# A depthwise convolution moves from VectorE to GpSimd, and a block of zero-writes moves later

## The reference

```python
def causal_depthwise_conv(u, w, b):          # u: 512 tokens x 768 channels, w: 4 taps
    out = lax.conv_general_dilated(u, w[:, None, :], window_strides=(1,),
        padding=[(CONV_WIDTH - 1, 0)], dimension_numbers=('NWC', 'WIO', 'NWC'),
        feature_group_count=u.shape[-1])
    return out + b

def first_block(x, w_in, conv_w, conv_b, ...):
    proj = jnp.einsum('bsd,de->bse', x, w_in[l])
    q, k, v, iq, ik, iw, z, xbc, dt_raw = jnp.split(proj, IN_SPLIT_POINTS, axis=-1)
    ...
    att = dsa_attention(q, k, v, iq, ik, iw * INDEXER_SCALE, topk)   # top 128 keys per query
    xbc = jax.nn.silu(causal_depthwise_conv(xbc, conv_w, conv_b))    # inside ssd_mixer
    ...
    mixed = jnp.einsum('bse,ed->bsd', jnp.concatenate([att, ssd], -1), w_out[l])
```

## Time and profile before

| what | value |
|---|---|
| median of three runs | 2731.35 us |
| the profiled execution, its own time | 2729.13 us |
| its span | 2727.3 us |
| TensorE busy | 2595.5 us (95%) |
| VectorE busy | 1299.9 us (48%) |
| ScalarE busy | 1090.7 us (40%) |
| GpSimd busy | 837.0 us (31%) |
| DMA | 318.80 MB, 117 GB/s on the mean |
| granted TensorE clock, mean | 0.978 |

### The profile page before, as it was taken

How to read it: one execution, slowest core, us unless ns; L and a number is a source line. 1 busy time by engine, 2 the same in 40 slices (tenths; PEclk the granted TensorE clock), 3 DMA queues, 4 the chain that set the end, 5 groups by cost and what they waited for, 6 DMA issues and landing times.

```text
span 2727.3 us, 30622 instructions
## 1 busy us (share of the span) xinstructions
PE 2595.5 (95%) x12190; PEld 2075.9 (76%) x12190; DVE 1299.9 (48%) x1841; ACT 1090.7 (40%) x1696; POOL 837.0 (31%) x354
## 2 busy tenths in 40 slices
PE   7998999999899999989999999999999999999997
PEld 6777787777676788878788888766888878788886
DVE  2895456777548646544431010576457353610113
ACT  2344235566426547333322122347374233322232
POOL 3300010000131344432234444321444432344344
PEclk9998989999999999999999999999999999999999
DMA  6242238899621233341223323221333331233332
GB/s 205 86 108 60 74 135 287 312 354 343 200 74 47 62 93 101 95 130 62 78 77 109 108 92 102 71 62 33 100 93 101 109 108 55 70 100 116 93 93 77
DMA packets 220078, 318.80 MB, mean 117 GB/s; under 512 B 17185, under 2 KB 176033, under 8 KB 219809
## 3 DMA queue, kind: packets, MB, share of 16 engines
q1 hardware_dynamic: 201184, 284.24, 32.7%
q10 hardware_dynamic: 16592, 24.72, 2.7%
q0 software_dynamic: 2160, 7.89, 0.8%
HBM read 301.06 MB, written 15.75 MB: 116 GB/s over the span
## 4 chain that ended last, share of the span: by engine, by line
PE 87%; DVE 8%; ACT 2%; issue 1%; DMA 1%; ACTq 0%; POOL 0%; DVEq 0%; SPq 0%
PE ps L639 80%; PE ps L790 4%; PE ps L651 3%; DVE stats L2061 1%; DVE rows L2071 1%; DVE pair_l L2356 1%; DMA rows<-in_x 1%; DVE x_lo L1987 1%; DVE xc L2217 0%; DVE shift L2090 0%; DMA xblk<-xs 0%; ACT pair_h L1665 0%; ACT w_hi L1438 0%; DVE rows L2083 0%; DVE qf L2447 0%
## 5 line engine op out<-in xcount | busy, mean ns | idle before, releaser
L603 POOL TENSOR_TENSOR w_lo<-w_raw,w_hi 128x1024 fp32r<-128x1024 f32 x331 | 814.8, 2472 | 1512.2 <-ACT w_hi L1438 1512.1
L639 PE MATMUL ps<-x_hi,w_hi 128*128 128x512 f32 x1624 | 656.4, 404 | 19.0 <-DVE x_lo L1987 16.5
L639 PE MATMUL ps<-x_lo,w_hi 128*128 128x512 f32 x1624 | 640.0, 394 | 0.0
L639 PE MATMUL ps<-x_hi,w_lo 128*128 128x512 f32 x1624 | 637.7, 393 | 0.0
L1438 ACT ACTIVATE w_hi<-w_raw 128x1024 fp32r<-128x1024 f32 x331 | 340.5, 1052 | 459.3 <-PE ps L639 447.8
L639 PEld LDWEIGHTS ps<-x_hi,w_hi 128*128 128x128 f32 x1624 | 308.1, 190 | 103.7 <-issue 19.4
L639 PEld LDWEIGHTS ps<-x_lo,w_hi 128*128 128x128 f32 x1624 | 307.7, 189 | 71.0
L639 PEld LDWEIGHTS ps<-x_hi,w_lo 128*128 128x128 f32 x1624 | 308.3, 190 | 67.1 <-issue 2.9
L2591 DVE TENSOR_TENSOR fhd<-fsg,ps 128x512 f32<-128x512 f32 x44 | 30.2, 687 | 391.6 <-PE ps L639 391.5
L2356 DVE TENSOR_TENSOR pair_l<-pair_raw,pair_h 128x2048 fp32r<-128x2048 f32 x84 | 189.8, 2288 | 47.4 <-ACT pair_h L1665 47.2
L1665 ACT ACTIVATE pair_h<-pair_raw 128x2048 fp32r<-128x2048 f32 x84 | 157.7, 1908 | 4.3 <-ACT yb L1680 2.8
(11 more groups left out here) (402 smaller groups left out, 4297.0 us busy)
## 6 DMA issues: line engine op xcount, KB each, us to landing
w_raw<-in_w_in SPq DMA_DIRECT2D x102, 512.0 KB, 3.7
w_raw<-in_ffn_wi SPq DMA_DIRECT2D x88, 512.0 KB, 3.6
pair_raw<-in_w_gate SPq DMA_DIRECT2D x56, 512.0 KB, 5.8
pair_raw<-in_w_up SPq DMA_DIRECT2D x56, 512.0 KB, 7.1
pair_raw<-in_w_down SPq DMA_DIRECT2D x56, 512.0 KB, 6.4
w_raw<-in_ffn_wo SPq DMA_DIRECT2D x44, 512.0 KB, 3.6
w_raw<-in_w_out SPq DMA_DIRECT2D x24, 512.0 KB, 3.6
kv_raw<-in_ckv_w SPq DMA_DIRECT2D x20, 512.0 KB, 4.5
```

The costliest lines, as they stand in the source:

```text
L603: pool.tensor_tensor(w_lo[:, slot, :], w_raw[:, slot, :], w_hi[:, slot, :].bitcast(F32), ALU.subtract).then_inc(lo_done, 1)
L639: ins = pe.matmul(o, a, b, start=first, stop=last)
```

## The change

The four taps of the convolution no longer run behind the barrier. ScalarE makes the first tap of chunk c in unit c of the attention (c = 0 to 5). [...] ScalarE waits for all six before the barrier. `xc1` moves to a place that three of the six raw slabs of the memory's weights had, so these have three places. The six small parameter loads move from just before the attention to the start. The zero-writes stand behind the third `low` instead of ahead of the first.

```diff
-    kv_raw = [place(f"kv_raw{i}", [P, SLAB], F32, early + 8 + 4 * i) for i in range(6)]
+    kv_raw = [place(f"kv_raw{i}", [P, SLAB], F32, early + 8 + 4 * i) for i in range(3)]
+    xc1 = place("xc1", [P, 6, T], F32, early + 20)
+    tap_p = place("tap_p", [P, T], F32, 28)
...
                     for f in range(20):
-                        if f >= 6:
-                            kv_used(f - 6)
+                        if f >= 3:
+                            kv_used(f - 3)
                         load_kv(f)
...
+            for n in range(RING):
+                low(n, n + 1)
             pool.wait_ge(blanked, 1)
             for b in range(BLOCKS):
                 pool.dma_start(xs[b * P:b * P + P, :], gain[:, :, :].rearrange("p a n -> p (a n)")[:, 0:ROW])\
                     .then_inc(cleared, 16)
-            for n in range(N_FIRST):
+            for n in range(RING, N_IN + 2):
+                low(n % RING, n + 1)
+            steps = 0
+            for c in range(6):
+                pool.wait_ge(s["taps0"], c + 1)
+                if c:
+                    pool.wait_ge(s["convolved"], c)
+                for back in (1, 2, 3):
+
+                    if steps:
+                        pool.wait_ge(tapped, steps)
+                    pool.tensor_scalar(tap_p[:, 0:T - back], pf[:, 8 + c, 0:T - back], taps[:, 3 - back, c:c + 1], None,
+                                       ALU.mult).then_inc(tapped, 1)
+                    steps += 1
+                    pool.wait_ge(tapped, steps)
+                    ins = pool.tensor_tensor(xc1[:, c, back:T], xc1[:, c, back:T], tap_p[:, 0:T - back], ALU.add)
+                    if back < 3:
+                        steps += 1
+                        ins.then_inc(tapped, 1)
+                ins.then_inc(s["convolved"], 1)
+            for n in range(N_IN + 2, N_FIRST):
                 low(n % RING, n + 1)
...
             act.dma_start(const[:, P:NCONST], A["tables"][:, P:NCONST]).then_inc(start, 16)
+            load((taps[:, :, 0:6], per_feature("conv_w", 0)),
+                 (tap_bias[:, 0:6], per_feature("conv_b", 0)),
...
             act.wait_ge(s["params_landed"], 16 * 6)
+            def first_tap(c):
+                if c < 6:
+                    act.activation(xc1[:, c, :], pf[:, 8 + c, :], ACT.Identity, scale=taps[:, 3, c:c + 1],
+                                   bias=tap_bias[:, c:c + 1]).then_inc(s["taps0"], 1)
+            attention(UNITS1, width1, sc1, pt1, by_head=True, beside=first_tap)
             split(1)
+            act.wait_ge(s["convolved"], 6)
             barrier()
-            for c in range(6):
-                act.activation(xc1[:, c, :], pf[:, 8 + c, :], ACT.Identity, scale=taps[:, 3, c:c + 1],
-                               bias=tap_bias[:, c:c + 1]).then_inc(s["taps0"], 1)
             act.activation(head_in[:, 3, :], head_in[:, 1, :], ACT.Exp).then_inc(s["gate_exp"], 1)
             softplus(sp[:, 2, :], sp[:, 1, :], sp[:, 4, :], sp[:, 3, :])
             for c in range(6):
-                act.wait_ge(s["convolved"], c + 1)
                 act.activation(xc1[:, c, :], xc1[:, c, :], ACT.Silu).then_inc(s["activated"], 1)
...
             softplus_start(x_sp, mag)
-            for c in range(6):
-                dve.wait_ge(s["taps0"], c + 1)
-                for back in (1, 2, 3):
-                    ins = dve.scalar_tensor_tensor(xc1[:, c, back:T], pf[:, 8 + c, 0:T - back], taps[:, 3 - back, c:c + 1],
-                                                   xc1[:, c, back:T], ALU.mult, ALU.add)
...
             softplus_end(x_sp, e_sp, u_sp, l_sp, tmp, dt)
```

More of the change, by code:

```diff
@@ L244, in build @@
     narrow_f = place("narrow_f", [20, T], F32, 64)
-    xc1 = place("xc1", [P, 6, T], F32, 79)
     xt1 = place("xt1", [P, NT, 512], F32, 46)
@@ L292, in kv_slab @@
         if f < 20:
-            return kv_raw[f % 6]
+            return kv_raw[f % 3]
         return kv_front[f - 20] if f < 22 else kv_beside if f < 26 else kv_tail[f - 26]
@@ L403, in build @@
         out_normalised, out_scaled, out_ready = sem("out_normalised"), sem("out_scaled"), [sem(f"out_ready{t}") for t in range(NT)]
-        blanked, cleared, scattered, block_stored, gathered = sem("blanked"), sem("cleared"), sem("scattered"), sem("block_stored"), sem("gathered")
+        blanked, tapped, cleared, scattered, block_stored, gathered = sem("blanked"), sem("tapped"), sem("cleared"), sem("scattered"), sem("block_stored"), sem("gathered")
         pair_landed = [sem(f"pair_landed{i}") for i in range(RAWS)]
@@ L1455, in high_parts, with attention @@
                 done.passed(transposed=KD)
-            def attention(units, width, sc, pt, by_head=False):
+            def attention(units, width, sc, pt, by_head=False, beside=None):
                 def exps(u):
@@ L1481, in attention @@
                             kv_store(u // 3)
+                        beside(u)
                     else:
@@ L1544, in _ @@
             act.dma_start(const[:, P:NCONST], A["tables"][:, P:NCONST]).then_inc(start, 16)
+            load((taps[:, :, 0:6], per_feature("conv_w", 0)),
+                 (tap_bias[:, 0:6], per_feature("conv_b", 0)),
+                 (head_in[:, 0, :], A["dt_bias"][0].partition_broadcast(P)),
+                 (head_in[:, 1, :], A["a_log"][0].partition_broadcast(P)),
+                 (head_in[:, 2, :], A["d_skip"][0].partition_broadcast(P)),
+                 (norm_w[:, :], per_feature("ssd_norm_w", 0)))
             def features(n, c, bank):
@@ L1601, in _ @@
                    .then_inc(mem_copied, 1)
[L1602 to L1608, removed]
-            act.wait_ge(s["params_landed"], 16 * 6)
+            act.wait_ge(s["params_landed"], 16 * 6)
+            def first_tap(c):
[3 more added lines that the diff above has]
+            attention(UNITS1, width1, sc1, pt1, by_head=True, beside=first_tap)
             split(1)
+            act.wait_ge(s["convolved"], 6)
             barrier()
-            for c in range(6):
-                act.activation(xc1[:, c, :], pf[:, 8 + c, :], ACT.Identity, scale=taps[:, 3, c:c + 1],
-                               bias=tap_bias[:, c:c + 1]).then_inc(s["taps0"], 1)
             act.activation(head_in[:, 3, :], head_in[:, 1, :], ACT.Exp).then_inc(s["gate_exp"], 1)
@@ L2213, in _ @@
             softplus_start(x_sp, mag)
-            for c in range(6):
-                dve.wait_ge(s["taps0"], c + 1)
-                for back in (1, 2, 3):
-                    ins = dve.scalar_tensor_tensor(xc1[:, c, back:T], pf[:, 8 + c, 0:T - back], taps[:, 3 - back, c:c + 1],
-                                                   xc1[:, c, back:T], ALU.mult, ALU.add)
-                    if back < 3:
-                        link(ins)
-                ins.then_inc(s["convolved"], 1)
             softplus_end(x_sp, e_sp, u_sp, l_sp, tmp, dt)
```

## The result

The kernel after takes 2715.22 us on the median (2712.03 to 2717.11, five runs); the kernel before took 2729.89 beside it (2725.19 to 2732.07, five runs). The ratio is 0.9945, 95% interval 0.9933 to 0.9958: by it 15.0 us less, between 11.5 and 18.3 (the two medians differ by 14.7). Forecast were 9.1 us. The profiled execution of after took 2717.11 us (span 2715.3), 12.0 less than that of before; it is the slowest of the five.

The account below looks back on a forecast made before the run. TensorE, busy 95% of the span, was taken to bound the kernel, so only its waits can give time back. -4.7 + 3.0 - 7.4 = -9.1 us gave 2722.2 us against the median, range 2715 to 2728.

Parts of the forecast that it names:

- Start: At the load of x: without the zero-writes x lands at 13.7 us in place of 18.41, 4.7 us earlier.
- What follows on TensorE waits for nothing until the attention, so the shift is kept: From x's landing to the attention: TensorE keeps the whole 4.7 us of the earlier landing.
- The upper bound of 7: At the start: 7 us gained if x gets all 325 GB/s of three queues and some of their mutual losses.
- Attention: In the search's tail: GpSimd's instructions hold five of VectorE's, 5.0 us late; 3 us reaches TensorE, bounds 0 and 8.
- slack of 2.1: In the attention at unit 10: VectorE can be 2.1 us late before TensorE waits.
- Raw places: At the kv loads: three raw places cost nothing; if the cover fails, 4.5 us once.
- Behind the barrier: Between kv(9) and the transposes: TensorE's idle 6.44 us goes, transposes give another 1.0; 7.4 us gained, between 6.4 and 8.5.
- Contention: Rival in the attention: VectorE's tail held twice per instruction (+8), start gives only 3 us; 2729 us, chance 0.09.
- starved weights: Rival at slabs 4 to 6: moved zeros delay a slab, 4 us lost; 2726, chance 0.11 together with x unchanged.
- an x that the zeros do not hold: Rival at the start: x's queue was not held, start gives 0; 2727, chance 0.11 together with starved weights.
- GpSimd last to arrive: Rival at the barrier: convolution outlasts the attention, slower from 2.25 us per instruction; upper price +9.7, 2741; chance 0.06.
- The range's lower end, 2715: Whole kernel: all terms at their better bound (-7, 0, -8.5) give the low end of the 8-in-10 range.

Follow-up runs that it names:

- e1: The kernel before with only the zero-writes moved behind the third low part; 2722.77 us, ratio 0.9977.
- e4: The kernel before with 32 transposes of already loaded data between the two halves of x; 2726.24 us, ratio 0.9993.
- e2: The kernel after with the zero-writes back ahead of the first low part; 2724.32 us, ratio 0.9982 to the kernel before.
- e3: The kernel before with three raw places for the memory's weights in place of six; 2730.36 us, ratio 1.0004.
- e5: The kernel after with each of GpSimd's 18 multiplications done twice; 2729.15 us, ratio 0.9996 to the kernel before.
- e10: The kernel before with only kv(9) put behind the transposes and the cumulated sums; 2730.72 us, ratio 1.0006.
- e7: The kernel after with kv(9) put behind the transposes and cumulated sums, run twice; 2707.79 and 2710.16 us, ratios 0.9921 and 0.9924 to the kernel before.
- e6: The kernel after with ScalarE making the 18 products and GpSimd only adding; 2715.71 us, ratio 0.9942 to the kernel before.
- e8: The kernel after with 40 transposes of constants ahead of the first half of x; 2715.93 us, ratio 0.9944 to the kernel before.
- a0: The kernel after run once more, unchanged; 2715.65 us, ratio 0.9945 to the kernel before.
- e9: The kernel after with the edits of e6, e7 and e8 in one; 2712.48 us, ratio 0.9936 to the kernel before.

## Why the prediction was wrong

The direction and all three places were right; 9.1 us was too little. By its own steps:

- **Start, the term that failed: forecast 4.7 us, measured 6.4 in the pair of traces.** The landing was right, 13.7 forecast and 13.73 measured, and so was its cause (e1: the zeros alone do it). The step "What follows on TensorE waits for nothing until the attention, so the shift is kept" took only the landing. It had priced the first half's transposes, at either clock, and never the second half's, which went from 3.67 to 1.97 us (e4 shows why). The first half landed at 9.94, later than the 9.3 that the sum asked for, but its transposes took 3.7 us and not 4.4, and in after they ended as the second half landed. And the 18.41 us of before was one draw of a quantity that varied: 18.4 to 21.2 over five traces with the zeros first. The attention's first scores come at 149.3 to 152.7 in the four of them without added transposes, and at 141.8 to 143.0 in the nine with the zeros later; the means differ by 9.0 us. That is an estimate from few traces, and above what e1 kept in the end: 6.3 us, interval 3.8 to 8.7. In e2 and e3, which started last, the part behind the output projection was 3 to 4 us shorter than in before. The upper bound of 7 does not come out of its own reason either: 1.74 MB at 325 GB/s from 5 us on land at 10.4, 8.1 us earlier; the earliest landing in any trace is 12.69.
- **Attention: forecast +3.0, measured +2.0** (0.0 to 2.1 over the nine traces with the convolution on GpSimd, e5 without its wait, against 78.73). The mechanism was right, down to which instructions are exposed and that MAX8 is not (0.69 us for 512 columns before and after). But the tail was held 2.7 us, not 5.0: the rows fit an instruction that is held only for what is left of GpSimd's, and some fall between two. The forecast's slack of 2.1 was a bit large; by the table it is about 1.4. The multiplication took 1.57 us where 1.2 was assumed, so GpSimd needed 52.9 us, not 47, and ended 17 us before it was needed.
- **What the two cited pages said.** GpSimd was held by VectorE too: 1.76 and 1.89 us for 1.57. The Trainium skill (SBUF — State Buffer, Who interferes with whom) has the lock work both ways, and the trace agrees. GpSimd's multiplication took 1.57 us, longer than its two-input addition. The Trainium skill (GPSIMD Engine Reference, Engine selection) calls one-input instructions there roughly line-rate, which the prediction estimated at 0.43 us for 512 columns; the measurement contradicts it.
- **Raw places: forecast 0, measured 0** (e3).
- **Behind the barrier: forecast -7.4, measured -8.4,** and 8.0 in e2. The 6.44 us of idle time went, kv(8) and kv(9) took 9.78 in place of 10.12, and the transposes gained 1.4 us, not 1.0. They start 0.11 us apart and the last lasts 0.27, 2.35 us for 20; the forecast divided 0.83 us by six and so counted a sixth of the last one's length with each. Part of e2's gain is gone by the output projection: from kv(8) to there it took 92.1 us, 6.7 less than before, where after took 8.8 less. e10 and e7 show that the last to arrive had become TensorE, as forecast.
- **Sum.** -6.4 + 2.0 - 8.4 = -12.8 against the forecast's -9.1; with -0.4 and +1.2 later it is the pair's -12.0. The last 3 us to the 15.0 of the ratio lie within its interval (11.5 to 18.3). A part of them may be the early landing in the one trace of before; that is not settled.
- **The rivals.** Contention, starved weights (no wait for a slab before 60 us) and an x that the zeros do not hold are ruled out. GpSimd last to arrive does not happen at 1.47 us per instruction (52.9 us for 36), but the point at which the gain is gone was about right (e5). Its +9.7 us was not: it gave all 36 instructions 2.5 us, though the text next to it keeps the additions at half a low part; with 18 at 2.5 and 18 at 1.3 the convolution ends at 226.1, in time. The range's lower end, 2715, stood for all three terms at their better bound, 15.5 us together. The time came close to it though the three terms sum to only 12.8 in the pair of traces, so this nearness is not the mechanism of that bound.

## What to carry to other kernels

When a transfer lands earlier, ask what the engine behind it did while it waited: work right behind idle time can take twice as long (3.67 us for 1.97 here), and closing the gap can give that back too. When a wait is removed, look at once at what stands ahead in the waiting engine's own queue, since reordering it may pay only then (e7 against e10). A stage that gets shorter need not make the kernel shorter: follow the gain to a later common point (e6 and e8). And a landing time read from a single trace is a draw: look for a second trace, or widen the range towards the side on which there is room.

## What the runs showed of the hardware

- TensorE's 16 transposes behind idle time took 3.67 us (starts 0.21 us apart), 16 behind work 1.97 (0.11 apart). In before the rows give a granted clock of 1.00 for both; in e2, e3 and e10 they give 0.50 for the long ones. Early in a trace the lengths say what the column may not.
- GpSimd's multiplication of 128 x 512 floats by a per-partition scalar took 1.57 us, its addition of two tiles of that size 1.09.
- How long VectorE is held by GpSimd depends on the phase more than on the amount: 18 multiplications more (e5) held the tail 0.4 us, in after 2.7.
- The same code from the output projection to the end (the expert blocks and all behind them) took 2394.3 to 2402.0 us over all kernels. Summing, over stretches of 10 us behind 320 us, the part by which the granted clock lies under 1, that is 39 and 41 us in the two e7, 43 in e2 and 44 in e3 (2396.9 and 2397.7 us), 46 in before, e1 and e6 (2400.5 or 2400.6), 50 in a0, e9 and after (2401.7 to 2402.0). The long ones go with the low clock; what sets it off is open.
